# Summing the modulation weights over the partitions: a moving block of 128 columns of ones, or one column

## The reference, cut to what matters

```python
c_act = jax.nn.silu(c)                                   # 1 x 1024
for i in range(2):
    mods = jnp.split(c_act @ w_ada[i] + b_ada[i], 6, -1) # w_ada[i]: 1024 x 6144
    sh1, sc1, g1, sh2, sc2, g2 = mods
    u = x * (1.0 + sc1) + sh1
    y = gla_mixer(u, ...) if i == 0 else chunk_attention(u, ...)
    x = layer_norm(ALPHA * x + (1.0 + g1) * y, ...)
    u = x * (1.0 + sc2) + sh2
    y = squared_relu_mlp(u, ff_w1[i], ff_w2[i])
    x = layer_norm(ALPHA * x + (1.0 + g2) * y, ...)
```

## Time and profile before

| | us |
|---|---|
| median of 3 runs | 1144.07 |
| lowest and highest run | 1142.17, 1144.33 |
| the profiled execution, its own time | 1143.43 |
| its span (first to last instruction) | 1141.1 |
| TensorE matmuls busy (PE) | 1032.3 (90%) |
| TensorE weight loads busy (PEld) | 923.4 (81%) |
| VectorE (DVE) busy | 824.7 (72%) |
| ScalarE (ACT) busy | 504.7 (44%) |
| mean granted TensorE clock | 0.969 of full |

### The profile page before, as it was taken

How to read it: one execution, slowest core, us unless ns; L and a number is a source line. 1 busy time by engine, 2 the same in 40 slices (tenths; PEclk the granted TensorE clock), 3 DMA queues, 4 the chain that set the end, 5 groups by cost and what they waited for, 6 DMA issues and landing times. The chain is left out here.

```text
span 1141.1 us, 16510 instructions
## 1 busy us (share of the span) xinstructions
PE 1032.3 (90%) x6736; PEld 923.4 (81%) x6736; DVE 824.7 (72%) x1118; ACT 504.7 (44%) x669; POOL 64.1 (6%) x138
## 2 busy tenths in 40 slices
PE   0789988999999899868999999699999989999996
PEld 0778967899989688747898989488888879999995
DVE  4668898888779788747856556856876567777775
ACT  0464524333433644535334343354345555555553
POOL 3001110000000111100000000100000000000000
PEclk9989998999999999988999999799999999999999
DMA  9858775778778377322655555253343434555651
GB/s 340 334 197 302 276 298 196 287 291 304 283 275 320 105 289 247 129 74 74 240 189 180 195 177 197 89 170 138 111 144 116 148 130 152 200 171 186 198 172 68
DMA packets 35049, 227.91 MB, mean 200 GB/s; under 512 B 4096, under 2 KB 4224, under 8 KB 10144
## 3 DMA queue, kind: packets, MB, share of 16 engines
q1 hardware_dynamic: 25232, 167.01, 42.0%
q0 software_dynamic: 9744, 59.87, 14.0%
HBM read 225.82 MB, written 1.05 MB: 199 GB/s over the span
## 5 line engine op out<-in xcount | busy, mean ns | idle before, releaser
L1387 DVE TENSOR_TENSOR weight_lo<-weight_raw,weight_hi 128x2048 fp32r<-128x2048 f32 (+3 forms) x187 | 361.4, 1936 | 115.1 <-ACT weight_hi L991 115.0
L416 PE MATMUL ps<-act_hi,weight_hi 128*128 128x256 f32 x1400 | 354.2, 291 | 11.4 <-ACT gla_q L995 5.6
L991 ACT ACTIVATE weight_hi<-weight_raw 128x2048 fp32r<-128x2048 f32 (+2 forms) x168 | 299.9, 1786 | 128.9 <-PE ps L416 97.3
L416 PE MATMUL ps<-act_lo,weight_hi 128*128 128x256 f32 x1400 | 349.0, 287 | 0.0
L416 PEld LDWEIGHTS ps<-act_hi,weight_hi 128*128 128x128 f32 x1400 | 274.4, 196 | 23.0 <-issue 13.4
L416 PEld LDWEIGHTS ps<-act_lo,weight_hi 128*128 128x128 f32 x1400 | 274.7, 196 | 3.4 <-issue 1.0
L416 PE MATMUL ps<-act_hi,weight_lo 128*128 128x256 f32 x1400 | 186.8, 283 | 0.0
L416 PEld LDWEIGHTS ps<-act_hi,weight_lo 128*128 128x128 f32 x1400 | 175.5, 191 | 0.2
L1407 DVE SCALAR_TENSOR_TENSOR ada_acc<-ada_raw,c_act,ada_acc 128x2048 f32<-128x2048 f32 x42 | 98.6, 2349 | 10.2 <-DMA ada_raw<-ada 8.8
L416 PE MATMUL ps<-weight_hi,mlp_lo 128*128 128x512 f32 x256 | 101.8, 398 | 0.0
L416 PE MATMUL ps<-weight_hi,mlp_hi 128*128 128x512 f32 x256 | 101.6, 397 | 0.0
(11 more groups left out here) (311 smaller groups left out, 1263.0 us busy)
## 6 DMA issues: line engine op xcount, KB each, us to landing
weight_raw<-weights SPq DMA_DIRECT2D x144, 1024.0 KB, 5.0
ada_raw<-ada POOLq DMA_DIRECT2D x48, 1024.0 KB, 6.5
weight_raw<-weights SPq DMA_DIRECT2D x23, 512.0 KB, 3.6
row_g<-ln_rows POOLq DMA_DIRECT2D x4, 512.0 KB, 5.4
row_b<-ln_rows POOLq DMA_DIRECT2D x4, 512.0 KB, 7.7
att_bias<-rel_bias POOLq DMA_DIRECT2D x16, 128.0 KB, 3.5
square<-ada_rows POOLq DMA_DIRECT2D x3, 512.0 KB, 3.8
dev<-x_in SPq DMA_DIRECT2D x1, 1024.0 KB, 10.5
```

Source lines behind the costliest of these rows:

```text
L416: return e.matmul(o, a, b, start=start, stop=False, skip_group_check=True)
L991: e.activation(weight_hi[h][:, 0:size], weight_raw[r][:, 0:size], ACT.Copy).then_inc(hi_full[h], 1)
L1387: ins = e.tensor_tensor(weight_lo[h][:, c], weight_raw[r][:, c], weight_hi[h][:, c].bitcast(F32), ALU.subtract)
```

## The change

The moving operand of `mods_of` becomes the first column of `ones_sq`, and the output one column of the bank. The number of matmuls, their stationary tiles, their order and every semaphore stay as they were. The column that VectorE reads has the same sum in it.

```diff
                 for i in range(n):
-                    last = e.matmul(bank(w)[:, i:i + P], a[:, (first + i) * P:(first + i + 1) * P], ones_sq[:, :],
+                    last = e.matmul(bank(w)[:, i:i + 1], a[:, (first + i) * P:(first + i + 1) * P], ones_sq[:, 0:1],
                                     start=True, stop=True, skip_group_check=True)
                 last.then_inc(mods_summed, 1)
```

## The result

The changed kernel takes **1147.35 us** (median of 20 runs, 1145.61 to 1151.62), the kernel before 1143.53 us (20 runs beside them, 1141.03 to 1149.74). The ratio is 1.0029, with a 95% interval of 1.0017 to 1.0041. The medians lie 3.8 us apart and the ratio stands for 3.3 us: a small slowdown, but its interval leaves out 1. The profiled execution took 1147.55 us with a span of 1145.2 us, against 1143.43 and 1141.1, and its mean granted clock was 0.965 against 0.969.

A forecast was written before the change was run, and what follows sets the result against it. TensorE was taken to bound the kernel wherever it doesn't wait. Clock terms 2.4 + 1.3 + 1.0 + 0.3 = 5.0 us, less 0.2 from shorter blocks, gave +4.8 on 1143.43: 1148.2 us, range 1142.8 to 1150.7.

The forecast's parts named there:

- Pace at full clock: L612's blocks at full clock: loads set the pace, 0.107 us per record; m3 gains 0.15 us, sc0 0.08.
- Pace at half clock: Most of m0: loads hold the pace at half clock too, about 0.21 us per record, so almost nothing is won.
- m0, +2.4: First block: clock rises only within the following projection, delaying it 2.1 us; m0 itself ends 0.3 later; +2.4 us.
- m3, +1.3: Block m3 and its tail: one 3.4 us half-clock stretch would lose 1.6 us; taken as +1.3 since the clock may hold.
- sh0, +1.0: Behind block sh0: clock falls, projection g3 loses 0.5 to 1.6 us at half clock, 0.1 us slack; +1.0 us.
- sc0, sh1, sc1, +0.3: No fall at sc0, TensorE idles anyway behind sh1 and sc1; +0.3 us for a slower start of the output projection.
- loads hold the clock, the time stays: Rival, all blocks: weight loads keep TensorE's clock, so no change, 1143.1 or 1143.7 us; chance 0.38.
- Only m0 pays: Rival: sums amid dense work keep the clock, only m0 fails to raise it; +2.2 us, 1145.6 us; chance 0.13.
- Faster: Rival, at m3, sc0 and m0: pace falls below a load of 0.107 us; 1140.2 us at half the pace; chance 0.04.

The follow-up runs named there:

- e8: Kernel before plus unused matmuls around m0 and in TensorE's wait before k1, VectorE taking m0's sum before splitting the second weight chunk: 1143.00 us, ratio 0.9991.
- e1: Kernel before with one moving column in m0 alone, the other five blocks keeping 128: 1149.67 us, ratio 1.0040.
- e2: Kernel before with one moving column in every block but m0, which keeps 128: 1146.53 us, ratio 1.0013.
- e6: Changed kernel with unused 128-column matmuls added, 14 ahead of m0 and 12 behind it: 1145.51 us, ratio 1.0005 against the kernel before.

## Why the prediction was right, and where it was not

I had forecast 1148.2 us, with the loss in TensorE's clock and none in the blocks; it came to 1147.35, inside the range, slower by 0.33% between the medians (0.29% by the ratio), and the loss lay in TensorE's clock, at two of the three places where the forecast had it. The steps:

- **Pace at full clock: right.** m3's 32 records begin (3.63 - 0.25) / 31 = 0.109 us apart, where I said 0.107. The blocks gave back 0.11 us each, against my 0.15 and 0.08. The 25 ns that I cited from the Trainium skill's page "TensorE: Matmul & The Clock Gate", section "Back-to-back issue gap", is its figure for the gap of single matmuls; the trace shows over four times that with a new load each. I had cited it too narrowly: the same section says that in a stream of loads and matmuls both set the spacing, and the page's section "LDWEIGHTS (loading the stationary operand)" gives columns / 1.2 in ns for a load. For 128 columns that makes 107 ns, an estimate from the page. With it the trace agrees at full clock (106 to 109); at half clock it shows 213.
- **Pace at half clock: right.** (6.96 - 0.35) / 31 = 0.213 us in m0.
- **m0, +2.4: right.** ScalarE's read came 2.17 us later, or 2.54 from m0's start. The half clock under the projection lasted 4.8 us (42.6 to 47.4), which at 0.48 per us is 2.3. I had used 2.1 for the delay. The 0.48 came from counts that I read wrongly as records begun: 15 and 29 begin in the two stretches of the earlier trace rows, not 16 and 31. The ratio, and with it the 0.48, comes out the same.
- **m3, +1.3: right in kind, a little small.** The fall came in every profiled execution with one column there (five of five), and cost 9.51 - 7.96 = 1.55 us: the 1.6 that I had for a full stretch (with the 8 and 16 records that do begin in the two stretches of the earlier trace rows it would have been 1.7). My discount for a clock that may hold was not needed.
- **sh0, +1.0: this step failed.** The fall came (146.4 to 149.8) and the end wasn't moved. I took VectorE's L1706 at 150.99 for the one that waits, with ScalarE's two copies up to 150.89 as its input and 0.1 us of slack. That reading was wrong: after the change L1706 starts at 153.92, before those copies, which start at 154.53. It starts when VectorE is done with two chunks of L1407, and by `out_residue` in the code it reads the copies of the head before. What needs g3 first is ScalarE's L1125 (149.69 to 150.29 before, 154.03 to 154.63 after), and VectorE reads its result only at 153.93, now 156.87: 3.6 us of slack, of which 2.2 are left. TensorE's own next wait, for VectorE ahead of the expansion of the sums (L622), was 1.79 us and is now 0.38; TensorE's lost time went into it. Rows of before, and then of after:

```profile
146.27 4.80 DVE L1407 SCALAR_TENSOR_TENSOR ada_acc<-ada_raw,c_act,ada_acc 128x2048 f32<-128x2048 f32 x2
151.87 1.13 PE L622 MATMUL ps<-ada_acc,ones_sq 128*128 128x512 f32 x2 [1.79 <-DVE mods L1414]
```
```profile
149.20 4.80 DVE L1407 SCALAR_TENSOR_TENSOR ada_acc<-ada_raw,c_act,ada_acc 128x2048 f32<-128x2048 f32 x2
154.80 1.13 PE L622 MATMUL ps<-ada_acc,ones_sq 128*128 128x512 f32 x2 [0.38 <-DVE mods L1414]
```

  I should have followed the slowed products to their real first reader and to TensorE's own next wait, and not to the instruction nearest in time.
- **sc0, sh1, sc1, +0.3: nothing.** No fall behind sc0, as expected. From sc1's start to the output projection it is 5.41 us (502.35 to 507.76) against 5.42.
- **What I hadn't priced: +0.8 between gla_gk's read and sh0.** It isn't the change's own. TensorE waits 5.6 us before k1, the clock falls, and the half clock then lies over the products of k1 for longer or shorter. Before it ended 3.6 us after k1's start (74.2 - 70.65), in the second execution of before 5.7 us (76.4 - 70.7), in the changed kernel 5.3 us (78.1 - 72.81); the column gk-sh0 reads 89.59, 90.50 and 90.36. In e8, with no half clock there, it reads 88.52. An execution of either kernel can have it: two of before's three do.

My two errors (sh0 +1.0 too much, this one 0.8 too little) happened to cancel in the profiled execution, so the sum of +4.8 against +4.1 looks better than its parts. What the change itself costs in these two executions is m0's 2.2 to 2.5 and m3's 1.55, 3.7 to 4.1 us. That the medians lie 3.8 us apart is no proof of this sum. In some executions before pays 1.6 us at m0 or 2.5 to 2.8 us behind sh0 as well, and how often is not known for those without a trace. The parts don't add up in the medians either: e1 alone has 5.2 us and e2 2.0. So the mechanism and the size at m0 and m3 are shown, and the agreement of the total with the forecast is partly luck.

Of the rivals, "loads hold the clock, the time stays" had the largest chance next to the forecast. It is refuted by m0, by m3 and most directly by e6. The literal reading of the Trainium skill's page "TensorE: Matmul & The Clock Gate", Part 1 ("The HAM clock gate"), and of its table "Why this matters for your kernels", by which a train of loads is a busy engine, fails on the same row: loads busy for 3.40 of 3.40 us, then half clock. "Only m0 pays" is refuted by the wait in e2. "Faster" needed a pace well below 0.107; the shortest is 0.106, in sh0 and sc0.

## What to carry to other kernels

Before you shrink the moving side of a matmul whose weights change each time, see whether the records are already a load apart; if they are, nothing is to be had. Columns that cost no time may still be what TensorE's clock is kept up with, and the bill then comes in the product behind. Follow each slowed stretch to the next wait of the same engine: at m0 and m3 another engine stood waiting and it was paid in full, at sh0 TensorE itself had 1.79 us to spare and the first reader 3.6, and it was free.

## What was unexpected about the chip

- **The clock stayed up where it would not come up.** With 64 columns per load m0 never raised the clock, while m3 with the same block kept it. With one column m3 lost it as well. With 64 or 96 columns sh0 lost it too, with a wait of 1.4 us behind it. 96 columns raised it in m0 at 38.6 and it was gone at 42.0, behind a wait that was also longer than before.
- **Where the clock steps fall relative to the work differs from one execution to the next**, and in the profiled executions it makes 1.6 us behind m0, up to 1 at k1, and 2.5 to 2.8 behind sh0. The start of m0, when its inputs have landed, differs as well (32.2 to 34.8 us), and so does the part behind m3 (770.9 to 774.5); its 3.6 us were not followed to a cause, so what makes up the whole spread of about 10 us stays open. A single pair of traces would have put 0.8 us down to the change wrongly. Cutting many executions at the same events separates the terms that repeat (m3: 7.96 to 7.98 with 64 columns or more, 9.51 to 9.54 with one) from those that don't.
